# A fifth pair of K tiles by seven products in the second feed-forward's down projection, and its weight splits further ahead

## The reference

```
def swiglu(x, w_gate, w_up, w_down):
    return (jax.nn.silu(x @ w_gate) * (x @ w_up)) @ w_down
...
        x = x + 0.5 * swiglu(rmsnorm(x, ff2_norm[l]), ff2_w_gate[l], ff2_w_up[l], ff2_w_down[l])
    return rmsnorm(x, final_norm)
```

## Time and profile before

| | |
|---|---|
| median of 3 runs | 1210.38 us (1210.21 to 1210.63) |
| the profiled execution's own time | 1210.59 us |
| its span, first to last instruction | 1208.6 us |
| TensorE busy | 1199.2 us, 99% of the span |
| VectorE busy | 937.7 us, 78% |
| ScalarE busy | 677.3 us, 56% |
| DMA, mean | 187 GB/s |
| granted TensorE clock, mean | 0.999 of full speed |

### The profile page before, as it was taken

One profiled execution on the slowest core, in us unless ns is written; L12 is line 12 of the kernel. 1 busy time (PEld: TensorE's weight loads), 2 busy tenths in 40 slices (PEclk: granted clock), 3 DMA queues, 4 the chain that ended last, 5 costly groups with the idle time before them and its releaser, 6 DMA issues.

```text
span 1208.6 us, 16281 instructions
## 1 busy us (share of the span) xinstructions
PE 1199.2 (99%) x6100; PEld 1010.0 (84%) x6100; DVE 937.7 (78%) x1386; ACT 677.3 (56%) x970; POOL 42.1 (3%) x85
## 2 busy tenths in 40 slices
PE   9999999999999999999999999999999999999997
PEld 7888888888887888888888888888888888888886
DVE  5999997756676666888978677786887777677797
ACT  7566655546666354665656554656544464566561
POOL 2000002100000000000010001000001000000000
PEclk9999999999999999999999999999999999999999
DMA  7676566755445556665557556566566444766552
GB/s 274 196 209 192 183 206 209 246 174 152 145 142 190 174 175 209 181 198 179 192 181 196 184 195 221 169 195 196 187 215 214 151 140 139 241 181 194 186 189 72
DMA packets 150909, 225.83 MB, mean 187 GB/s; under 512 B 8152, under 2 KB 85984, under 8 KB 150832
## 3 DMA queue, kind: packets, MB, share of 16 engines
q1 hardware_dynamic: 148304, 216.10, 56.3%
q0 software_dynamic: 2512, 8.69, 2.6%
q10 hardware_dynamic: 16, 0.00, 0.0%
HBM read 223.72 MB, written 1.05 MB: 186 GB/s over the span
## 4 chain that ended last, share of the span: by engine, by line
PE 98%; DVE 0%; DMA 0%; ACT 0%; SPq 0%; DVEq 0%; issue 0%
PE ps L691 23%; PE ps L603 17%; PE ps L610 17%; PE ps L618 17%; PE ps L695 12%; PE ps L528 3%; PE ps L673 2%; PE ps L671 2%; PE ps L668 2%; PE ps L862 1%; PE ps L877 1%; DMA raw<-in_ff_w_gate_dram 0%; PE ps L1081 0%; PE ps L845 0%; PE ps L1051 0%; PE ps L800 0%
## 5 line engine op out<-in xcount | busy, mean ns | idle before, releaser
L1776 DVE TENSOR_TENSOR wl<-raw,wh 128x1024 fp32r<-128x1024 f32 (+1 forms) x405 | 476.7, 1198 | 85.0 <-ACT wh L1152 83.2
L1152 ACT ACTIVATE wh<-raw 128x1024 fp32r<-128x1024 f32 (+1 forms) x405 | 408.0, 1034 | 53.4 <-PE ps L618 12.4
L691 PE MATMUL ps<-XT,wh 128*128 128x512 f32 x1216 | 423.0, 393 | 0.0
L695 PE MATMUL ps<-XT,wl 128*128 128x256 f32 x1216 | 338.8, 279 | 0.0
L691 PEld LDWEIGHTS ps<-XT,wh 128*128 128x128 f32 x1216 | 227.8, 187 | 51.7
L695 PEld LDWEIGHTS ps<-XT,wl 128*128 128x128 f32 x1216 | 229.0, 188 | 0.2
L603 PE MATMUL ps<-wh,XT 128*128 128x512 f32 x510 | 202.5, 397 | 0.0
L610 PE MATMUL ps<-wl,XT 128*128 128x512 f32 x510 | 199.3, 391 | 0.4 <-DVE wl L2617 0.3
L618 PE MATMUL ps<-wh,XT 128*128 128x512 f32 x510 | 158.0, 391 | 0.0
L610 PEld LDWEIGHTS ps<-wl,XT 128*128 128x128 f32 x510 | 95.9, 188 | 20.4 <-DVE wl L2617 1.6
L603 PEld LDWEIGHTS ps<-wh,XT 128*128 128x128 f32 x510 | 95.8, 188 | 20.1 <-issue 0.7
(11 more groups left out here) (339 smaller groups left out, 1395.0 us busy)
## 6 DMA issues: line engine op xcount, KB each, us to landing
raw<-in_ffn_w_gu_dram SPq DMA_DIRECT2D x88, 512.0 KB, 4.2
raw<-in_w_in_dram SPq DMA_DIRECT2D x56, 512.0 KB, 4.1
raw<-in_ff_w_up_dram SPq DMA_DIRECT2D x44, 512.0 KB, 4.6
raw<-in_ff_w_down_dram SPq DMA_DIRECT2D x44, 512.0 KB, 3.8
raw<-in_ffn_w_down_dram SPq DMA_DIRECT2D x44, 512.0 KB, 4.3
raw<-in_ff_w_gate_dram SPq DMA_DIRECT2D x40, 512.0 KB, 4.2
raw<-in_gla_w_in_dram SPq DMA_DIRECT2D x24, 512.0 KB, 4.2
raw<-in_moba_w_in_dram SPq DMA_DIRECT2D x24, 512.0 KB, 4.6
```

Source lines behind the costliest of these rows:

```text
L691: e.matmul(o, wh_of(j)[:, w], XT[:, kt, :, :].rearrange("p a n -> p (a n)"), start=kt == 0, stop=False)
L695: ins = e.matmul(o[:, 0:256], wl_of(j)[:, w], XTH[:, kt, :], start=False, stop=kt == kts - 1)
L1152: e.activation(wh_of(j)[:, 0:m], source(j), ACT.Copy).then_inc(S("wh"), 1)
L1776: e.tensor_tensor(wl_of(j)[:, 0:m], source(j), wh_of(j)[:, 0:m].bitcast(F32), ALU.subtract).then_inc(S("wl"), 1)
```

## The change

f2 gets a fifth seven: pair 10 (narrow pair 8, the last one) is added to `SEVEN`. The list in `plan_down` changes with it: pair 1's half 1 moves from d0 to d1, pair 10's eights go, no eight is put between the fourth seven and the fifth, and the K index at which a product bank is closed follows the last eight. And in f2 the stretch in which nine chunks are split ahead begins at the gate product of narrow pair 7, the last but one, and no longer at the first chunk of the down projection. Other feed-forwards keep their order: their stretches begin where they did.

```
-SEVEN = {"f1": (4, 5, 6, 7), "f2": (1, 2, 3, 7), "f3": (1, 2, 3), "f4": (1, 2, 3, 7)}
+SEVEN = {"f1": (4, 5, 6, 7), "f2": (1, 2, 3, 7, 8), "f3": (1, 2, 3), "f4": (1, 2, 3, 7)}
...
-                if s:
+                if s and len(rest) > 1:
                     normal(*rest.pop(0))
                 seven(s)
...
-            blocks[f"{f}d0"] = (len(blocks), begin, len(chunks), 512, 22)
+            blocks[f"{f}d0"] = (len(blocks), begin, len(chunks), 512, 2 * eight[-1] + 2)
...
-            blocks[f"{f}d1"] = (len(blocks), begin, len(chunks), 512, 22)
+            blocks[f"{f}d1"] = (len(blocks), begin, len(chunks), 512, 2 * eight[-1] + 2)
...
-        stretches = [(mixed[f][0][2], last_seven(f) - 3) for f in FFNS]
+        def before_down(f):
+            return blocks[f"{f}g{NARROW[-2][0]}"][1] if f == "f2" else mixed[f][0][2]
+
+        stretches = [(before_down(f), last_seven(f) - 3) for f in FFNS]
...
-                        for t in block(f"{f}g{c0}"):
+                        for t in block(f"{f}g{c0}", 0, MORE):
...
-                        for t in block(f"{f}u{c0}"):
+                        for t in block(f"{f}u{c0}", 0, MORE):
```

## The result

The changed kernel took 1214.57 us in the median of 7 runs (1212.85 to 1214.87) against 1210.38 before (1210.03 to 1210.66, 7 runs); the ratio is 1.0026, with a 95% interval from 1.0016 to 1.0035. The quotient of the two medians themselves is 1.0035, the upper end of that interval. The kernel is slower. In a second job (experiment 1, `again`), 11 executions of the same kernel had a median of 1213.09, ratio 1.0021 (1.0012 to 1.0030). The execution that was profiled took 1213.32, 2.7 us more than the profiled one of before; its span is 1211.4 in place of 1208.6.

The account below looks back on a forecast made before the run. TensorE was taken as the bound, VectorE just ahead of it. Three matmuls removed, -0.68, plus delays of 2.4, 0.65 and 0.2 gave +2.6 us on 1210.38: 1213.0 us, range 1211.4 to 1214.4.

Parts of the forecast that it names:

- the three places: TensorE's forecast waits: the second product's bank, the first split behind the gather, the transposes of the normalised X.
- the ledger: VectorE's account up to f2's gather: 7.01 us more work, 2.50 of gaps filled, gather at 611.78 instead of 607.27.
- The filled gaps: VectorE's gaps behind product copies and ahead of the gather take in 2.50 us; 0.51 and 0.52 behind ScalarE stay.
- The first: TensorE waits 1.5 us for the bank of the down projection's second product, whose addition ends at 572.6.
- The second: TensorE waits 0.9 us more in d1 for the first split behind the gather; delay in all 2.4 us.
- The third: TensorE waits 0.65 us at the transposes of the normalised X, plus some 0.2 for their second piece.
- Cheaper: Rival, 23%: the same three waits but smaller, VectorE's account off by 0.5 to 1 us; 1212.3 in the middle.
- no waits: Rival, 6%: TensorE stays the only bound and the three matmuls are simply gone; 1209.7 us.
- Loads too late: Rival, 15%: late loads leave the narrow pairs' gaps unfilled in time, up to +1.86 us; about 1214.2.
- The drain's rule: Each of VectorE's 12 added operations would cost about 0.08 us more, 1 us on top; left out of the sum.

Follow-up runs that it names:

- experiment 1: Also `again`: the changed kernel run again in a second job with no edit; median 1213.09 us, ratio 1.0021.
- experiment 6: The changed kernel with one redundant VectorE addition of 128x1024 just ahead of f2's gather; 1214.47 us.
- experiment 9: Also `early_four`: the kernel before, with four sevens in f2 but the nine chunks' lead beginning at narrow pair 4; 1210.64 us, ratio 1.0002.
- experiment 3: Also `lead_only`: the changed kernel without the fifth seven, the longer lead from narrow pair 7 kept; 1211.81 us, ratio 1.0010.
- experiment 8: Also `sums_on_gpsimd`: the changed kernel with the lead from narrow pair 4 and f2's row sums moved from VectorE to GpSimd; 1219.27 us, ratio 1.0074.
- `f4_five_no_lead`: The kernel before, f2 unchanged, with a fifth seven in f4 and its lead still beginning at the down projection; 1214.43 us, ratio 1.0032.
- `fifth_pair_only`: The changed kernel with the fifth seven in f2, but the lead beginning at the down projection as before; 1215.60 us, ratio 1.0041.

## Why the prediction was right

The mechanism was right: VectorE became the later engine, and TensorE waited in the three places that were named. On the size, the forecast was +2.6 us, 1213.0. The profiled executions show +2.7, the second job +2.5 (1213.09). The first job's median of 1214.57 lies 0.2 us above the upper end of the range (1214.4), while its ratio of 1.0026 would put the time at 1213.5, inside it.

**The bound and the ledger.** The gather was forecast for 611.78 and came at 611.82, the first split behind it for 617.9 where TensorE's wait ended at 618.02, the normalised X for 626.97 and the transposes began at 627.07. This closeness is in part luck. From the anchor at the narrow pairs to the gather, VectorE took 58.53 us before; in `again` it took 62.64 (from 548.49 to 611.13), 4.1 more, where the ledger said 4.5. In the first profile a load that landed late gave just the missing 0.4 back.

**The filled gaps.** The right ones went: those behind copies were filled and those behind Silu stayed, but for the 0.96 in place of 0.51. Their size is where the 0.4 us lie. The ledger took the work from starts, where the next operation can begin before the end of the one ahead, but the gaps from their rows, which count from that end. The first one, before and in `again`:

```profile
551.62 0.41 DVE L1901 TENSOR_TENSOR SGf<-ps,SGf 128x256 f32<-128x256 f32 x1
...
552.84 0.69 DVE L1968 TENSOR_TENSOR SGf<-SGf,ps 128x512 f32<-128x512 f32 x1
```

```profile
554.77 0.74 DVE L1904 TENSOR_TENSOR SGf<-ps,SGf 128x256 f32<-128x256 f32 x2
555.62 0.69 DVE L1971 TENSOR_TENSOR SGf<-SGf,ps 128x512 f32<-128x512 f32 x1
```

1.22 us became 0.85, 0.37 saved for a gap of 0.28. In the same way 0.13 gave 0.22, 0.90 gave 1.01, 0.55 gave 0.65 and the 0.64 ahead of the gather 0.73. That is 2.98 us in place of 2.50, and 7.01 - 2.98 = 4.0 agrees with the 4.1 measured. So the extra work was sized well, and the filled gaps 0.5 too low.

**The three waits.** Their places and their releasers were right. The first was forecast as 1.5; by starts it was 1.45 (572.77, where the second product could have followed 0.46 behind the row at 570.86). The second was forecast as 0.9 and was 0.69 (0.53 + 0.16), since the waits and restarts ahead of it had already delayed TensorE by 1.8 and not 1.5. The delay in all, down to this wait, was forecast as 2.4 and is 2.5 (618.02 for 615.5). The third added 0.65 and 0.2 in the forecast; measured on the transposes the delay is 2.5 + 0.7 (the removed matmuls) = 3.2 for the first piece, with 0.3 more for the second.

**What was not in the sum.** The restart after each wait, 0.11 us, and the 0.10 and 0.14 us at the first product. They use up slack of TensorE, but don't come on top at the end: at the transposes TensorE waits for VectorE, whose own queue sets their time. What is left there is 0.1 us at their start (627.07 for 626.97) and 0.1 in their second piece (0.28 for 0.2).

**The rivals.** *Cheaper* and *no waits* did not happen. That TensorE at 99% is the only bound is refuted by experiment 6, where an operation on an engine at 78% cost its full 1.14 us. So the rule of the Trainium skill in Perfetto Trace Analysis, Identifying the Most-Contended Engine, taken over the whole span, points the wrong way here; its own remark on kernels with several regimes (section Optimization Strategy of the same page) fits what was seen. Between 580 and 600 us of the kernel before, TensorE was busy for all of 20 us and VectorE for 19.80. *Loads too late* had a mechanism that exists, at a quarter of its price: 0.45 us in one profile and none in the next. The drain's rule that the prediction weighed (the Trainium skill, VectorE: DVE Perf Modes, section The DRAIN you can't avoid), that a next operation starts only when the pipe is empty, was not borne out in the changed kernel either: four splits of 1.22 us took 4.63. The same section adds, which the prediction left out, that a next operation starts earlier where it is not held. The splits, 1.14 us apart, agree with that.

**What stays open.** The changed kernel's 1214.57 in the first job lies 1.3 us above its profiled execution and 1.5 above `again`. Many kernels' executions fall into two groups some 1.9 us apart (last section); 4 of those 7 lie within 1214.57 to 1214.87. That they belong to the upper group is argued from their times; they were not profiled. The shares of the two halves of the change are measured; that each microsecond of VectorE's work counts is shown ahead of the gather alone.

## What to carry to other kernels

Before trading work of the bounding engine for work of one that feeds it, count the feeder's gaps in the stretch itself, not over the whole span, and only those gaps that the new order can fill: here 3.5 us of gaps, 2.5 of them fillable (3.0 by starts), stood against 7.0 us of new work to save 0.7. Take work and gaps in the same measure, from start to start. Splitting further ahead showed no cost where it began early (experiment 9), and cost a wait where the extra splits stood just ahead of an operation that frees a bank (experiment 3). Read a wait's cost from the starts of the rows, since a wait's own row can understate it by a quarter of a microsecond, and look at the granted clock behind a wait of several microseconds (experiment 8).

## What the runs showed of the hardware

- **A stage of dense matmuls comes at two speeds.** In `lead_only`'s profiled execution, 1.6 us above its own median, the excess lies in f4's narrow products alone, where nothing was changed. First before, then `lead_only`, the line of the 128x512 matmuls with min/median/max ns, first and last start:

```profile
L691 PE MATMUL ps<-XT,wh x288: 389/391/476, 1043.3 to 1143.7; 128*128 128x512 f32 x144
```

```profile
L694 PE MATMUL ps<-XT,wh x288: 389/398/477, 1044.2 to 1146.5; 128*128 128x512 f32 x144
```

  100.4 us in the one, 102.3 in the other, with the granted clock at full in both and no wait in the list. Three more profiled executions from an upper group show the same stage length once each: `early_four` in f1 (31.8 to 134.0), `sums_on_gpsimd` in f1 (31.9 to 134.2) and `f4_five_no_lead` in f4 (1043.3 to 1145.6). In the other profiles these stages last 100.4 us. It comes in kernels with and without the change. What sets it was not found.
- **GpSimd and VectorE slow each other.** A 128x128 float32 addition took GpSimd 0.46 us with VectorE idle beside it (497.75 and 498.29 in `sums_on_gpsimd`) and up to 1.50 beside VectorE's operations, against VectorE's 0.28. Three VectorE operations beside it took 20 to 32% longer; a split that began just ahead of GpSimd's first operation (568.78) kept its 0.69.
- **TensorE restarts slowly.** The first 128x512 matmul behind a wait was followed after 0.34 us in place of 0.23 (572.77 and 618.02 in the changed kernel).
- **A wait of 3.6 us lowered TensorE's clock, waits of up to 1.7 us didn't.** Behind the wait of 3.59 us in `sums_on_gpsimd` the granted clock was 0.50 for some 6 us, which cost 2.8 us more. Behind those of 1.3 us in the changed kernel and of 1.6 and 1.7 in `fifth_pair_only` it stayed at full.
